# Two attention layers of a fused transformer kernel: half-row score products, own counts for split weights, and another order of the second attention

## What is computed

```
# layer 0: 8 heads; each has two query-key products of depth 64, and one value of width 128
logits = einsum('bqhcd,bkhcd->bhcqk', q * 64 ** -0.5, k)          # c = 0, 1
p = softmax(where(mask, logits - slope * dist, -inf))
o = einsum('bhqk,bkhd->bqhd', p[:, :, 0] - lam * p[:, :, 1], v)
h = rmsnorm(o, subln_g) * (1 - lambda_init) @ w_o

# layer 1: 8 heads; a part of depth 128 per head and a rotated part of depth 64
kv_a = x @ w_kv_a;  c_kv = rmsnorm(kv_a[..., :256]);  k_rope = rope(kv_a[..., 256:])   # shared by heads
k_nope, v = split(c_kv @ w_kv_b)
q_nope, q_rope = split(rmsnorm(x @ w_q_a) @ w_q_b);  q_rope = rope(q_rope)
logits = (q_nope . k_nope + q_rope . k_rope) * 192 ** -0.5
h = softmax(where(mask, logits, -inf)) @ v @ w_o
```

## Time and profile before

| | us |
|---|---|
| median of 3 runs | 736.33 |
| the 3 runs | 739.26, 736.12, 736.33 |
| the profiled execution | 735.09 |
| its span, first to last instruction | 733.3 |
| PE busy | 688.5 (94%) |
| DVE busy | 330.9 (45%) |
| ACT busy | 212.5 (29%) |
| POOL busy | 133.0 (18%) |

### The profile page before, as it was taken

How to read it: one execution, slowest core, us unless ns; L and a number is a source line. 1 busy time by engine, 2 the same in 40 slices (tenths; PEclk the granted TensorE clock), 3 DMA queues, 4 the chain that set the end, 5 groups by cost and what they waited for, 6 DMA issues and landing times. The chain is left out here.

```text
span 733.3 us, 10061 instructions
## 1 busy us (share of the span) xinstructions
PE 688.5 (94%) x3657; PEld 389.5 (53%) x3657; DVE 330.9 (45%) x674; ACT 212.5 (29%) x418; POOL 133.0 (18%) x145
## 2 busy tenths in 40 slices
PE   7999899879999999999979898987999999999993
PEld 5989788544433334345546797855333434334551
DVE  4756844772342423224253457467243332423326
ACT  4668452412111211111145237241211111111111
POOL 6003010141201001011019570014120101001000
PEclk9999999999999999999999999999999999999998
DMA  9980029847999999999996009374999999999991
GB/s 310 382 333 2 1 100 423 354 191 296 414 421 421 421 422 420 422 422 421 423 416 267 0 9 421 151 306 182 339 422 420 421 420 422 422 422 421 420 413 68
DMA packets 40359, 237.65 MB, mean 324 GB/s; under 512 B 3824, under 2 KB 4256, under 8 KB 15232
## 3 DMA queue, kind: packets, MB, share of 16 engines
q1 hardware_dynamic: 39408, 235.64, 78.8%
q10 hardware_dynamic: 576, 1.05, 0.4%
q0 software_dynamic: 336, 0.44, 0.3%
HBM read 236.06 MB, written 1.05 MB: 323 GB/s over the span
## 5 line engine op out<-in xcount | busy, mean ns | idle before, releaser
L564 PE MATMUL psum<-ring,work 128*64 128x512 f32 (+2 forms) x1296 | 232.4, 509 | 7.1 <-DVE work L1943 7.1
L564 PEld LDWEIGHTS psum<-ring,work 128*64 128x64 f32 (+1 forms) x1296 | 94.6, 139 | 142.1 <-issue 118.0
L564 PE MATMUL psum<-ring,scratch 128*64 128x512 f32 x512 | 116.9, 598 | 3.7 <-ACT scratch L1409 3.7
L1985 DVE TENSOR_TENSOR scratch<-psum,scratch 128x256 f32<-128x256 f32 x32 | 13.6, 425 | 183.8 <-ACT scratch L1405 183.8
L2061 POOL COPY work<-work 128x512 f32 x60 | 39.1, 654 | 314.2 <-PE psum L564 298.1
L1398 ACT ACTIVATE x_T_rounded<-psum,small 128x512 fp32r<-128x512 f32 x64 | 43.8, 687 | 109.7 <-DVE scratch_rounded L1966 77.9
L564 PEld LDWEIGHTS psum<-ring,scratch 128*64 128x64 f32 x512 | 33.9, 136 | 68.8 <-issue 63.6
L1405 ACT ACTIVATE scratch<-psum 128x256 f32<-128x256 f32 x32 | 12.3, 384 | 195.6 <-PE psum L564 195.6
L564 PE MATMUL psum<-ring_rounded 128*128 128x256 f32 (+1 forms) x214 | 66.1, 309 | 0.0
L564 PE MATMUL psum<-ring_rounded,x_T_rounded 128*128 128x512 f32 x192 | 60.9, 398 | 1.0 <-DVE work_rounded L1814 0.9
L564 PE MATMUL psum<-x_T_rounded,scratch_rounded 128*128 128x512 f32 x128 | 56.7, 443 | 0.9 <-issue 0.7
(11 more groups left out here) (253 smaller groups left out, 868.6 us busy)
## 6 DMA issues: line engine op xcount, KB each, us to landing
ring<-in_moe_w_gate SPq DMA_DIRECT2D x64, 1024.0 KB, 15.5
ring<-in_moe_w_up SPq DMA_DIRECT2D x64, 1024.0 KB, 19.6
ring<-in_moe_w_down SPq DMA_DIRECT2D x64, 1024.0 KB, 20.1
ring<-in_diff_w_qkv SPq DMA_DIRECT2D x5, 2048.0 KB, 19.6
ring<-in_diff_w_o SPq DMA_DIRECT2D x1, 4096.0 KB, 14.6
ring<-in_mla_w_o SPq DMA_DIRECT2D x1, 4096.0 KB, 35.9
ring<-in_mla_w_q_b SPq DMA_DIRECT2D x1, 2304.0 KB, 29.5
ring<-in_mla_w_kv_b SPq DMA_DIRECT2D x1, 2048.0 KB, 28.2
```

What stands on the lines that cost most here:

```text
L564: return pe.matmul(dst, lhsT, rhs, start=start, stop=stop, skip_group_check=True)
L1985: dve.tensor_tensor(h_sb, psum[:, 6, FF:2 * FF], act_s, ALU.mult).then_inc(m["h_ready"], 1)
```

## The change

Four things change.

1. **Half-row score products.** In both attentions the depth-64 products use 64 partitions of both operands instead of 128 with zeros. The two products of a pair (c = 0 and 1 of a head in layer 0, two neighbouring heads in layer 1) lie in the lower and the upper half of the partitions and write to two banks. They stand next to each other in PE's list. The zeroed copies, their memsets on POOL and the waits for them go; a query group of layer 0 is one copy of 128 partitions.
2. **Own counts.** `wo_lower` and the last chunk's `lower` wait for the upper part that they read (`WO_SPLIT`, `LAST_SPLIT`), and `squares(0, 4)` stands ahead of `move(7)` in DVE's list.
3. **First eighth and query part of the second attention.** The first low-rank product takes the eight slices of x in the order `A_ORDER`, and waits for each by itself. The second product of keys and values comes after the transposes of the normalised queries, and the rotated query products ahead of the transposes of the other low-rank result. ACT and DVE follow that order.
4. **Heads and output.** Scores of layer 1 are made for two heads at a time, on four banks. Half of the output products, those of heads 0 to 3, are done in the loop after heads 6 and 7 and behind the last value; the other half follows.

The diff, cut:

```diff
-B_BANKS = (4, 5, 0, 1, 6, 7, 4, 5, 2, 3, 5, 6)
+B_BANKS = (4, 5, 0, 1, 6, 7, 4, 5, 2, 3, 5, 4)
+SCORE_BANKS = (0, 1, 6, 7)
-MOVED = (2, 3, 4, 6, 7, 8)
+MOVED = (1, 2, 3, 4, 5, 6)
+WO_SPLIT, LAST_SPLIT = (21, 24, 25, 28, 29, 30, 31, 32), (22, 23, 26, 27)
+A_ORDER = (0, 2, 1, 3, 4, 6, 5, 7)
...
+                    banks = [psum[:, 2 * (h % 2) + c, :] for c in range(2)]
+                    rows = [slice(c * DH, (c + 1) * DH) for c in range(2)]
                     for c in range(2):
-                        bank = psum[:, 2 * (h % 2) + c, :]
-                        mm(bank[:, 0:3 * P], slope[:, h % 2, :], dist_b[:, :], True, False)
-                        mm(bank[:, 0:P], qz[:, h, c, 0:P], kT[:, h, 0:P], False, False)
-                        mm(bank[:, P:3 * P], qz[:, h, c, P:SEQ], kT[:, h, :], False, True).then_inc(s["sc_ps"], 1)
+                        mm(banks[c][:, 0:3 * P], slope[:, h % 2, :], dist_b[:, :], True, False)
+                    for c in range(2):
+                        mm(banks[c][:, 0:P], qT[rows[c], h, 0:P], kT[rows[c], h, 0:P], False, False)
+                    for c in range(2):
+                        mm(banks[c][:, P:3 * P], qT[rows[c], h, P:SEQ], kT[rows[c], h, :], False, True)\
+                          .then_inc(s["sc_ps"], 1)
...
+                def low_rank(bank, w, t, n):
+
+                    for i, k in enumerate(A_ORDER):
+                        if bank == 2:
+                            pe.wait_ge((mq["x_act"], mq["x_dve"])[i % 2], i // 2 + 1)
+                        last = mm(psum[:, bank, 0:n], xT[:, k, t * P:(t + 1) * P], w[:, k, :], i == 0, i == KD - 1)
                     last.then_inc(mq["a_ps"], 1)
...
+                low_rank(2, qa, 0, QR)
+                low_rank(3, qa, 1, QR)
                 pe.wait_ge(ld_kva, 16)
+                low_rank(0, kva, 0, KVR + ROPE)
                 pe.wait_ge(mq["c_ready"], 2)
+                transpose_c(c_q, QR // P, 4)
+                low_rank(1, kva, 1, KVR + ROPE)
...
+                pe.wait_ge(mq["c_ready"], 4)
+                transpose_c(c_kv, KVR // P, 6)
...
+                def scores(first):
+
+                    heads = (first, first + 1)
+                    if first >= 4:
+                        pe.wait_ge(*s("sc_read", first - 2))
+                    banks = [psum[:, SCORE_BANKS[h % 4], :] for h in heads]
+                    rows = [slice(i * ROPE, (i + 1) * ROPE) for i in range(2)]
+                    for h, bank in zip(heads, banks):
+                        mm(bank[:, 0:P], qnT[:, h, 0:P], knT[:, h, 0:P], True, False)
+                        mm(bank[:, P:3 * P], qnT[:, h, P:SEQ], knT[:, h, :], False, False)
+                    for h, bank, r in zip(heads, banks, rows):
+                        mm(bank[:, 0:P], qr[r, h, 0:P], krT2[r, 0:P], False, False)
+                    for h, bank, r in zip(heads, banks, rows):
+                        mm(bank[:, P:3 * P], qr[r, h, P:SEQ], krT2[r, :], False, True).then_inc(s["sc_ps"], 1)
 
                 scores(0)
-                scores(1)
                 group(10)
+                scores(2)
                 group(11)
-                scores(2)
...
                 for h in range(HEADS):
-                    if 1 <= h < HEADS - 3:
+                    if h in (1, 3):
                         scores(h + 3)
                     transposes(h)
-                    if h == 0:
-                        scores(3)
                     if h >= 1:
                         values(h - 1)
+                    if h == HEADS - 2:
+                        pe.wait_ge(*s("sc_read", 6))
+                    if h >= HEADS - 2:
+                        out_part(0, h - (HEADS - 2), range(4))
                 values(HEADS - 1)
+                for c in range(2):
+                    out_part(1, c, range(4))
                 pe.wait_ge(o_lo_ready, HEADS)
-                mla_out_projection()
+                for t in range(TT):
+                    for c in range(2):
+                        out_part(t, c, range(4, HEADS)).then_inc(wo_ps, 1)
...
-                    dve.wait_ge(w_hi_ready, 24 + h + 1 if l == 0 else 32 + h - 3)
+                    dve.wait_ge(w_hi_ready, WO_SPLIT[h] if l == 0 else 32 + h - 3)
...
                 wo_lower(0, wo_a, (1, 2))
+                squares(0, 4)
                 move(7)
                 lower(5, (2, 3))
                 wo_lower(0, wo_a, (3,))
-                squares(0, 4)
                 scale_heads(1, 0, 4)
```

159 lines of the change are left out of this document (68 added, 91 removed).

## The result

The changed kernel takes 728.87 us (median of ten runs, 727.18 to 733.79), the kernel before 738.09 us on the same chip (735.48 to 740.13). The ratio is 0.9889, with a 95% interval from 0.9872 to 0.9905: faster by 1.1%. The forecast had the sign, and missed the time: 722.7 us with a range up to 728. The saving is 9.2 us where 13.6 were forecast.

A forecast was written before the change was run, and what follows sets the result against it. Expert stages hang on when PE enters them, so attention savings should reach the end one for one: 3.7 + 2.6 + 6.9 + 0.4 = 13.6 us, from 736.33 to 722.7 us, range 719 to 728.

The forecast's parts named there:

- the 6.9: Second attention, x's transposes to group 0: 31.4 us falls to 24.5 without waits and at full clock, saving 6.9 us.
- Is all of it covered?: Second attention's start: whether copies and normalisation hide under PE's products, so that the whole 6.9 us is saved.
- Then groups 0 and 1, 4.3 us, stand before the first wait on the second copies.: Second attention: 4.3 us of PE work on groups 0 and 1 was taken to cover the second copies.
- Own counts and squares: First attention: PE's waits of 1.33 us for `move(7)` and 2.33 us for ACT both go, saving 3.66 us.
- Half-row scores: First attention: eight calls save 0.32 us each, 2.6 us in all, between -1.8 and 3.4.
- the two passages: Score calls: passing from half to full tiles costs 0.11 us more, two such passages a call, 0.22.
- Heads: Second attention: head 0's transposes 1.6 us later, head 6's 2.0 late, then 2.4 gained to the end; together 0.4 us.
- Half rows that don't overlap: Rival, score calls of both attentions: a call costs 1.52 us and the time is 728.7 us; chance 0.10.
- A surviving stall in the first attention: Rival: `move(7)` late behind POOL's chain, PE waits as before, ACT's `move(8)` too; 724.0 to 726.4 us; chance 0.10.
- Drained arrays: Rival: tile-shape changes drain the array; slower from 0.48 us a passage, 741 us at 0.7; chance 0.02.
- The clock that falls elsewhere: Rival: clock falls at second attention's start or second expert stage, 1.7 us each; 724.4, or 726.1 with both; chance 0.15.
- that execution's luck: Expert stages, earlier profile: first gate product 5.36 us in the first, 3.67 in the second; a clock fall costs 1.7 us.

The follow-up runs named there:

- the first experiment: Changed kernel with GpSimd's fifth remainder of the split weights held back until VectorE has rotated the shared key; 723.44 us, ratio to the kernel before 0.9793.
- the experiment above: Changed kernel with GpSimd's fifth remainder held back, value group 11 ahead of the scores of heads 2 and 3, two output products of head 0 in the head loop; 722.47 us.
- the experiment gives the early products: Changed kernel with all output products of the second attention back behind the last value product; 734.33 us, one run.

## Why the forecast was wrong, and where it was right

*The step that failed* is the answer to "Is all of it covered?", and in it the sentence "Then groups 0 and 1, 4.3 us, stand before the first wait on the second copies." Groups 0 and 1 do take 4.3 us. But what stands before the copies on DVE, the rotation, was neither priced nor set beside POOL's list. At 0.19 us a product the sentence would have held: in the first experiment the copies are done at 404.7 for a group 2 that is due near 407.2, 2.5 us to spare. The change moves the rotation up by 9.2 us (409.39 to 400.20) and POOL's remainders only by 4.3, with the expert stage (408.90 to 404.6). The 0.5 us between them became an overlap of 4.4. That cost 5.0 us of the 6.9: 3.24 of waiting and the rest, as far as the traces show, of clock. The first experiment, where the stretch shrinks by 7.15 us against before, shows that the 6.9 was right as the price of the work itself.

A row of before could have told it, and I had not put it into the sum. DVE's rotation of the queries there has a first product of twice the length, and only that one meets POOL's last product, which ends at 420.03:

```profile
419.46 0.84 DVE L429 TENSOR_TENSOR x_T<-x_T,cst 128x256 f32<-128x256 f32 x1
420.34 0.42 DVE L430 TENSOR_TENSOR scratch<-x_T,cst 128x256 f32<-128x256 f32 x1
```

*Level.* 736.33 us, from which I subtracted, was a median of three runs; the ten beside the changed kernel give 738.09. The miss of 6.2 us is 1.8 of level and 4.4 of saving. Without the lock the saving would have been 14.7 by the medians of the first experiment, for a forecast of 13.6.

*Own counts and squares*, 3.66: right in kind, the waits are gone. From head 3's scores to head 4's PE takes 27.89 us (50.18 to 78.07) instead of 32.26 (50.43 to 82.69); less one call's saving the waits were worth 4.1. The squares, named with the counts, were not needed.

*Half-row scores*, 2.6: right in kind, somewhat too high. The call ahead of head 3's transposes is 0.36 us shorter, but the transposes take 0.55 instead of 0.49 us, and from one call to the next the kernel gains 0.22 to 0.28. Eight are 2.1. The overlap is full and saves 0.65 us a call; the term that was mis-sized is the two passages, at 0.22 in the sum and 0.39 in the runs (0.65 less 0.26). Of these, 0.19 lie in the products themselves, by the starts above, 0.09 between the last mask product and the first half-row product (0.26 instead of 0.17), and the rest in what follows the call. The Trainium skill (TensorE: Matmul & The Clock Gate, packing small matmuls and LDWEIGHTS) had two rules that spoke against each other here: estimated by the concurrency of row groups the eight calls save 3.4, by the time of a weight load 1.8, and the runs came out at neither. The 0.86 us that the second gives for eight loads is near the 0.85 measured by chance: four instructions apart also take 0.85, and in the pairs two loads start 0.01 us apart, where the rule has 0.11 for each.

*Heads*, 0.4: 0.46 measured. Head 0's transposes come 8.49 us after the first scores instead of 6.68, so 1.8 later where 1.6 was said, with a wait of 0.83 where 0.9 was foreseen (the profile names no releaser for it; with the last value group moved ahead of it in the experiment above it is gone, as it should be if it was DVE's last value copy); head 6's are 1.9 late (2.0); from there to the end 24.49 us instead of 26.83, a gain of 2.3 (2.4), of which the experiment gives the early products 1.9.

*The rivals.* Half rows that don't overlap: excluded. A surviving stall in the first attention: excluded. Drained arrays: in part. A call pays 0.39 us for its two passages, near 0.2 each where the trace had 0.11, and far from the 0.48 each at which the kernel would have turned slower. The clock that falls elsewhere: in part. The fall at the start of the second attention went with its wait, as forecast, and came back with it when the early start was undone. The second expert stage's first gate product took 5.36 us here (3.67 in the earlier trace rows), so that execution's luck did not last. No rival had a new wait behind a shifted pair of lists, and with 0.60 on the forecast the range stopped at 728, 0.9 us short.

## What to carry to other kernels

When a change pulls one engine's list forward, put every instruction that moves beside what the other engines run at its new time, and for VectorE against GpSimd look at the operands: a small fp32 product, scaling or copy on SBUF alone can stand for a whole GpSimd instruction, while one with an operand in PSUM, or a reduction, passes. The cheap cure is to delay the GpSimd instruction that nobody waits for. Then look for the next collision, since a stall removed can let the next GpSimd piece start earlier: two lines were enough when the rotation kept its place, and two more were needed when it moved. And a saving in front of a wait that another engine sets is no saving: while the lock stood, 3.1 us of early start could be undone at no cost.

## What the runs showed of the hardware

- A VectorE product of 128x32 that takes 0.19 us took 4.50 beside a GpSimd instruction of 4.6 that had begun just before it, a scaling 3.70 and a copy 4.49 with one SBUF operand each. A product with an operand in PSUM took its 0.19, and two reductions of 128x128 from SBUF their 0.61 together, in the middle of a GpSimd instruction each. Where both engines ran short operations on SBUF they alternated: VectorE's of 0.42 took 0.84 each beside GpSimd's, which went from 0.74 to 0.80 in the first experiment.
- Half-row fp32 products side by side overlap fully: eight in the 0.85 us of four. Apart, four take 0.85 where four in whole rows take 0.66, and the difference lies at the passages: 0.10 between the first and the second, with no weights loaded ahead, and 0.09 behind the last. Both passages of a call cost 0.39 in all, so halves pay only in pairs side by side.
- After 3.24 us of idle time PE was granted 0.50, which is 1.2 of 2.4 GHz, from 411 to about 414.5, and with products of zeros in that time 1.00. After 1.45 us of idle time ahead of the low-rank products, in one run, it was 0.51 from 378 to 380, and the 16.55 us that the 48 instructions took then are 1.7 more than at 1.00.
